# Moving a batched 32x32 triangular solve from GpSimd to VectorE, in two parts between conv units, in a one-core encoder layer

## What is computed

```python
qkv = jax.nn.silu(causal_depthwise_conv(qkv_raw, w_conv))   # 12 groups of 128 channels
...
lower = jnp.where(strict, beta[..., :, None] * kk * decay, 0.0)
rhs = jnp.concatenate([v * beta[..., None], k * (beta * jnp.exp(g_cum))[..., None]], axis=-1)
sol = lax.linalg.triangular_solve(lower, rhs, left_side=True, lower=True, unit_diagonal=True)
```

## Time and profile before

| | us |
|---|---|
| time, median of 3 runs | 1889.42 |
| lowest, highest | 1881.87, 1894.11 |
| the profiled execution's own time | 1886.62 |
| its span, first to last instruction | 1885.0 |
| PE busy | 1781.2 (94%) |
| DVE busy | 888.3 (47%) |
| ACT busy | 473.6 (25%) |
| POOL busy | 167.2 (9%) |
| mean granted clock of PE | 0.966 of full speed |

### The profile page before, as it was taken

How to read it: one execution, slowest core, us unless ns; L and a number is a source line. 1 busy time by engine, 2 the same in 40 slices (tenths; PEclk the granted TensorE clock), 3 DMA queues, 4 the chain that set the end, 5 groups by cost and what they waited for, 6 DMA issues and landing times.

```text
span 1885.0 us, 22629 instructions
## 1 busy us (share of the span) xinstructions
PE 1781.2 (94%) x8387; PEld 1428.9 (76%) x8387; DVE 888.3 (47%) x1231; ACT 473.6 (25%) x861; POOL 167.2 (9%) x212
## 2 busy tenths in 40 slices
PE   6989878999899999999899979999999999999997
PEld 5867667888777767777678868888888888888876
DVE  6665465677544444443554345343333424333436
ACT  3324321222233343433321212111111111111101
POOL 1115371111100101010000000000000000000000
PEclk7899989999999999999999989999999999999998
DMA  7734546655623223160355310221021012102002
GB/s 246 216 98 151 166 136 194 190 173 175 184 58 83 78 79 100 46 172 23 139 168 178 90 56 23 67 67 45 23 67 56 24 54 67 54 13 67 23 0 101
DMA packets 208877, 186.13 MB, mean 99 GB/s; under 512 B 15481, under 2 KB 186618, under 8 KB 208826
## 3 DMA queue, kind: packets, MB, share of 16 engines
q1 hardware_dynamic: 201194, 157.91, 28.6%
q0 software_dynamic: 7632, 27.53, 3.8%
HBM read 140.58 MB, written 44.83 MB: 98 GB/s over the span
## 4 chain that ended last, share of the span: by engine, by line
PE 76%; DVE 4%; DMA 2%; issue 2%; POOL 2%; ACT 1%; SPq 0%; DVEq 0%; ACTq 0%; POOLq 0%
PE pm L886 34%; PE ps L886 16%; PE pm L1211 12%; PE aT L1080 3%; PE aS L1103 3%; PE aT L1091 1%; DVE asc L1753 1%; POOL pr L811 1%; POOL Xi L813 1%; PE gps L1025 1%; DVE a_raw L1751 1%; PE pm L1175 1%; DMA yst<-yb_d 1%; ACT w_hi L1258 1%; DVE tmp L1874 0%
## 5 line engine op out<-in xcount | busy, mean ns | idle before, releaser
L1534 DVE TENSOR_TENSOR w_lo<-w_raw,w_hi 128x1024 fp32r<-128x1024 f32 x105 | 129.1, 1230 | 549.5 <-ACT w_hi L1258 540.0
L886 PE MATMUL pm<-act_hi,w_hi 128*128 128x512 f32 x832 | 257.4, 391 | 4.0 <-DVE act_lo L1583 4.0
L886 PE MATMUL pm<-act_lo,w_hi 128*128 128x512 f32 x832 | 257.3, 391 | 0.0
L886 PE MATMUL pm<-act_hi,w_lo 128*128 128x512 f32 x832 | 256.6, 390 | 0.0
L886 PE MATMUL ps<-act_hi,w_hi 128*128 128x512 f32 x720 | 253.8, 434 | 2.4 <-DVE est L1636 2.4
L1258 ACT ACTIVATE w_hi<-w_raw 128x1024 fp32r<-128x1024 f32 x105 | 110.7, 1055 | 507.3 <-PE pm L886 493.0
L886 PE MATMUL ps<-act_lo,w_hi 128*128 128x512 f32 x720 | 228.7, 399 | 0.0
L886 PE MATMUL ps<-act_hi,w_lo 128*128 128x512 f32 x720 | 226.3, 396 | 0.0
L886 PEld LDWEIGHTS pm<-act_hi,w_hi 128*128 128x128 f32 x832 | 156.5, 188 | 36.9 <-issue 4.2
L886 PEld LDWEIGHTS pm<-act_lo,w_hi 128*128 128x128 f32 x832 | 156.7, 188 | 33.0
L886 PEld LDWEIGHTS pm<-act_hi,w_lo 128*128 128x128 f32 x832 | 156.5, 188 | 33.1
(11 more groups left out here) (277 smaller groups left out, 2117.7 us busy)
## 6 DMA issues: line engine op xcount, KB each, us to landing
w_raw<-in_w_in_dram SPq DMA_DIRECT2D x45, 512.0 KB, 5.4
w_raw<-in_w_ffn_in_dram SPq DMA_DIRECT2D x44, 512.0 KB, 3.8
a_raw<-in_w_ada_dram SPq DMA_DIRECT2D x32, 512.0 KB, 4.6
f_raw<-in_w_ffn_out_dram SPq DMA_DIRECT2D x22, 512.0 KB, 4.2
adab<-in_w_ada_dram SPq DMA_DIRECT2D x8, 1024.0 KB, 7.8
qkvb_d<-est POOLq DMA_DIRECT2D x12, 512.0 KB, 3.0
pk_d<-pk SPq DMA_DIRECT2D x8, 768.0 KB, 4.1
qkva_d<-est POOLq DMA_DIRECT2D x12, 512.0 KB, 4.5
```

What stands on the lines that cost most here:

```text
L886: ins = pe.matmul(dst[:, cols], wt[:, ds % 2, k, :], at[:, cols], start=(first and n == 0), stop=(last and n == 2))
L1534: dve.tensor_tensor(w_lo[:, ds % 2], w_raw[:, ds % NR], w_hi[:, ds % 2].bitcast(F32), ALU.subtract)\
```

## The change

The function `solve` moves from the POOL program into the DVE program. POOL keeps the stores of units 10, 11 and 12 and has nothing between them. DVE runs columns 0 to 11 (24 instructions) ahead of `conv(11)`, and columns 12 to 30 (38 instructions) ahead of the block of norms and `conv(12)`. The arithmetic, tiles and semaphores are the same.

```diff
             store_conv(9)
 
-            def solve(columns):
...
-            pool.wait_ge(xi_zero, 3)
-            pool.wait_ge(low_in, 16)
-            solve(range(0, 10))
-            store_conv(10)
-            solve(range(10, 22))
-            store_conv(11)
-            solve(range(22, BLK - 1))
-            store_conv(12)
+            for d in (10, 11, 12):
+                store_conv(d)
...
+            def solve(columns):
+
+                for j in columns:
+                    n, m = BLK - 1 - j, j + 1
+                    part = pr[:, 0:m * n].rearrange("p (c r) -> p c r", c=m)
+                    ch.link(dve.tensor_tensor(part, bc_mid(LB[:, j, j + 1:], m), Xi[:, 0:m, j:j + 1]
+                                               .broadcast_to([P, m, n]), ALU.mult))
+                    ins = dve.tensor_tensor(Xi[:, 0:m, j + 1:], Xi[:, 0:m, j + 1:], part, ALU.subtract)
+                    if j < BLK - 2:
+                        ch.link(ins)
+                    else:
+                        ins.then_inc(xi_ready, 1)
+
             dve.wait_ge(xT_stored, 16)
             for d in range(D_CONV, D_A):
+                if d == 11:
+                    dve.wait_ge(xi_zero, 3)
+                    dve.wait_ge(low_in, 16)
+                    solve(range(0, 12))
                 if d == D_A - 1:
+                    solve(range(12, BLK - 1))
                     for e in range(2):
                         dve.wait_ge(pre_read[e], 16)
```

## The result

| | before | after |
|---|---|---|
| median, us | 1886.20 (20 runs) | 1892.99 (20 runs) |
| lowest, highest | 1881.87, 1894.11 | 1889.85, 1898.20 |
| ratio after to before | | 1.0034, 95% interval 1.0025 to 1.0044 |
| profiled execution, own time | 1886.62 | 1889.85 |
| its span | 1885.0 | 1888.2 |

The change costs 0.34% of 1886 us, 6.4 us (4.7 to 8.3). It was forecast at +7.5 us; the median lies inside the range of 1887 to 1907. More runs of before have been added since the prediction, and its median went from 1889.42 to 1886.20, so the forecast of 1897 stands 4 us above the 1893 that was measured, while the forecast of the difference is off by 1. The profiled execution of the changed kernel was its fastest, so the two spans lie only 3.2 us apart.

A forecast was written before the change was run, and what follows sets the result against it. PE, busy 94%, was taken as the bound, reached through the store of unit 12. Solve, conv units and norms queued on DVE move that store from 275.0 to 282.5, +7.5 us: 1897 against the 1889.42 median, range 1887 to 1907.

The forecast's parts named there:

- the stretch: Start of unit 10's last DVE instruction to the small matmul with `asc` in slot 11: forecast 7.5 us longer.
- The price of an instruction: Each solve step on DVE: 0.194 us plus 0.00104 us an element, no penalty for short runs; 23.4 us together.
- Rival 1: Solve on DVE no cheaper than on POOL: 38 us in place of 23.4, +22 us, time 1911; chance 0.11.
- The contention on the norms: Block of norms on DVE: 3.5 us instead of 9.0, once POOL runs no tensor_tensor beside it.
- Rival 2: Block of norms on DVE stays at 9.0 us: +13.1 us, time 1902.5; chance 0.08.
- Rival 3: DVE cheaper on elements, 0.00064 us each: solve 19 us, sum +3.1 us, time 1892.5; chance 0.05.
- Rival 4: The inverse, not the store of unit 12, sets the end: -3.5 us, time 1886; chance 0.03.
- The clock: PE behind `Q_T0`: with the 5.5 us wait gone, matmuls no longer restart at the lower clock.
- The head of the chain: Store of unit 12 leads everything up to the slot 11 matmul; its issue moves from 275.0 to 282.5, +7.5 us.
- The margin of 2.1 us: PE reaches the slot 11 matmul at about 300.4, 2.1 us ahead of `asc`, so +7.5 us stands.

The follow-up runs named there:

- The two POOL runs: Changed kernel with chained GpSimd products added beside the solve's second part: 30 of 256 elements, ratio 1.0081 to before; 16 of 512 elements, 1908.87 us.
- part 2 behind unit 12: Changed kernel with columns 12 to 30 of the solve behind the last conv unit on DVE instead of ahead of it; ratio 1.0045 to the kernel before.

## Why the prediction was right

Step by step, relative to the end of unit 10's result on DVE (predicted 240.5; measured 238.2, since the stretch began 2.2 us earlier in this run):

| step | predicted | measured |
|---|---|---|
| solve, first part | 8.5 | 8.46 |
| a conv unit on DVE | 7.3 | 7.32 and 7.32 |
| solve, second part | 14.9 | 14.76 |
| block of norms, 9.0 before | 3.5 | 3.32 |
| from unit 10's result to the store of unit 12 | 42.0 | 41.8 |
| from that store to the slot 11 matmul | 19.95 | 19.67 |
| PE waits at unit 13 | about 4 | 4.06 |
| PE waits ahead of `Q_GQ` | about 20 | 18.5 |
| PE from `Q_GQ` to `Q_T0` | 16.9 | 17.3 |
| PE's wait ahead of `Q_T0` | almost none | none |
| PE from `Q_T0` to the slot 11 matmul, without its wait | 1.9 | 2.0 |
| the slot 11 matmul waits for `asc` | 2.1 | 1.46 |
| the stretch | +7.5 | +6.9 |

- **The price of an instruction** was right to 1%, from rows of 4, 64 and 512 elements for tiles of 31 to 256. The short inner runs, which no row had shown, cost next to nothing: 31 elements took 0.18 us as one run, and 0.21 as 31 runs of one. Rival 1 (+22) fell with this.
- **The contention on the norms** was right: with POOL idle they took 3.3 us. Rival 2 (+13.1) fell. The two POOL runs show the cause, which had only been argued: what was read off one row of 0.70 us is a DVE instruction waiting out one POOL instruction.
- **Rival 3** (cheaper elements) fell: 256 elements took 0.43 us, on the line.
- **Rival 4** (the inverse decides): `xi_ready` did come early, 268.8 against 274.7, and SP stood with it in hand until 283.4, as its queue says. Right.
- **The clock** was right for the stretch that it named: behind `Q_T0` PE ran at a granted clock of 1.00, where before the same work took 3.7 us (290.16 to 293.83) behind the wait. The lower clock behind the longer wait ahead of `Q_GQ` was left out: 0.84 on average up to `Q_T0`, against 0.91 in the earlier trace rows, and 17.3 us in place of 16.9.
- **The head of the chain** was put too simply. "If its issue moves by x, that matmul moves by x, unless PE itself arrives later": the clause carries the whole of it. In this change both sides move together, since the store and the readout of `Q_GQ` stand behind the same `conv(12)`. With part 2 behind unit 12 the store moved by 14.5 us and the end did not. What counts is when DVE has finished solve and `conv(12)` together, in whatever order.
- **The margin of 2.1 us** was 1.46 in one profile and 2.74 in the other. In the first, `asc` waited for the landing of `a_raw` (5.73 us, 295.64) and not, as said, for unit 15's weights, whose low part had started at 294.27 and would have let it start some 0.2 us sooner. In the second the low part came last, as said.

## What to carry to other kernels

A faster engine doesn't shorten a chain if the work lands ahead of something that others wait for. The solve took 46 us on GpSimd (waits included) and 23 on VectorE and was the worse there, because on GpSimd it ran beside VectorE's conv work, and on VectorE it was added to it. Ask of each instruction that moves what the engine would have done in that time; here VectorE had idle waits from 20 us upstream on, and the same instructions, most of them placed in these waits, turned +6.4 into -7.7.

The price per instruction can be had from rows of quite other tiles: two sizes give the line, a chained group gives the gap. What can't be had so is whom the work meets at its new place.

## What the runs showed of the hardware

- VectorE and GpSimd with tensor_tensor on SBUF, both chained: lockstep, one VectorE instruction to one GpSimd instruction. Beside GpSimd products of 256 elements a VectorE step took 0.67 to 0.69 us at 112 to 192 elements and 0.75 at 255 (0.46 without them); beside products of 512 elements 1.15 at 231 and 1.18 at 255. The larger VectorE tiles held GpSimd up a little, by about 1 ns an element.
- Where GpSimd had two such instructions back to back with no wait between them, a VectorE instruction of 0.30 to 0.42 us took 3.05 to 3.31 us in three runs. It waited out both, 2.5 us, although it had begun 0.3 to 0.5 us ahead of the first, while GpSimd issued the store of `ybst`. Once that was long enough to have been done (266.72 and 0.42 us against 267.22); why it was not isn't shown.
- GpSimd issued its stores at 238.83 and 254.60 while VectorE ran the solve, 0.53 us each; one at 225.47, with VectorE idle, took 0.60. No delay of the issue by tensor_tensor instructions could be seen.
